# A decoder layer on one core: the first tap of a convolution on ACT, the bias table mirrored by transfers through memory, and small parameters made elsewhere

## The reference, cut to what matters

```python
proj = jnp.einsum('bsd,de->bse', x, w_in[l])
z, xbc, dt_raw = proj[..., :o_z], proj[..., o_z:o_xbc], proj[..., o_xbc:o_dt]
...
xbc = jax.nn.silu(causal_dwconv(xbc, conv_w, conv_b))            # 4 taps, each channel by itself
dt = jax.nn.softplus(dt_raw.astype(jnp.float32) + dt_bias.astype(jnp.float32))
a = -jnp.exp(a_log.astype(jnp.float32)) * dt
...
bias = rel_bias.astype(jnp.float32)[t5_bucket(jnp.maximum(dist, 0))]   # dist = q - k
logits = jnp.where(dist >= 0, logits + bias.transpose(2, 0, 1)[:, None], -jnp.inf)
...
lam = (jnp.exp(jnp.sum(lq1 * lk1)) - jnp.exp(jnp.sum(lq2 * lk2)) + lam_init)
```

## Time and profile before

| | |
|---|---|
| median of 3 runs | 1021.77 us (1020.12 to 1022.16) |
| the profiled execution's own time | 1021.97 us |
| its span | 1019.8 us |
| PE busy in the span | 993.3 us, 97% |
| DVE busy | 524.5 us, 51% |
| ACT busy | 376.4 us, 37% |
| POOL busy | 56.3 us, 6% |
| DMA | 290.85 MB, mean 285 GB/s |

### The profile page before, as it was taken

One profiled execution on the slowest core, in us unless ns is written; L12 is line 12 of the kernel. 1 busy time (PEld: TensorE's weight loads), 2 busy tenths in 40 slices (PEclk: granted clock), 3 DMA queues, 4 the chain that ended last, 5 costly groups with the idle time before them and its releaser, 6 DMA issues.

```text
span 1019.8 us, 15454 instructions
## 1 busy us (share of the span) xinstructions
PE 993.3 (97%) x6370; PEld 711.6 (70%) x6371; DVE 524.5 (51%) x1049; ACT 376.4 (37%) x687; POOL 56.3 (6%) x53
## 2 busy tenths in 40 slices
PE   8999999999999999999999999999999999999994
PEld 7998999999999999998974444444444444444432
DVE  6899455675769966855677222322223222222223
ACT  5665435556577744455321211121112111211112
POOL 0000202324200000000010000000000000000000
PEclk9999999999999999999999999999999999999998
DMA  8564534333344555658837999999999999999972
GB/s 305 188 226 146 185 123 167 124 125 125 125 166 166 181 192 182 233 207 350 347 141 280 419 419 421 420 419 420 420 418 420 420 420 420 421 420 419 420 326 83
DMA packets 41653, 290.85 MB, mean 285 GB/s; under 512 B 4712, under 2 KB 5872, under 8 KB 6896
## 3 DMA queue, kind: packets, MB, share of 16 engines
q1 hardware_dynamic: 40800, 284.62, 70.6%
q0 software_dynamic: 784, 5.24, 1.3%
HBM read 288.78 MB, written 1.06 MB: 284 GB/s over the span
## 4 chain that ended last, share of the span: by engine, by line
PE 86%; DVE 10%; issue 2%; DMA 1%; ACT 1%; SPq 0%; ACTq 0%; DVEq 0%
PE stream L1548 24%; PE stream L1876 22%; PE stream L1900 11%; PE stream L1573 8%; PE work L1865 6%; DVE w_lo L972 3%; DVE acc L1008 3%; PE stream L1824 2%; PE stream L1828 1%; PE stream L1826 1%; PE stream L1830 1%; DMA raw<-in_wdense 1%; PE work L1675 1%; PE work L1651 1%; PE work L1851 1%
## 5 line engine op out<-in xcount | busy, mean ns | idle before, releaser
L972 DVE TENSOR_TENSOR w_lo<-raw,w_hi 128x1024 fp32r<-128x1024 f32 x142 | 171.4, 1227 | 57.1 <-ACT w_hi L668 57.0
L1876 PE MATMUL stream<-ring,xg 128*64 128x512 f32 x640 | 197.0, 592 | 0.8 <-issue 0.8
L668 ACT ACTIVATE w_hi<-raw 128x1024 fp32r<-128x1024 f32 x142 | 147.1, 1052 | 53.2 <-DMA raw<-in_wdense 36.4
L1548 PE MATMUL stream<-xT_hi,w_hi 128*128 128x256 f32 x560 | 161.3, 288 | 1.4 <-DVE w_lo L972 1.4
L1548 PE MATMUL stream<-xT_lo,w_hi 128*128 128x256 f32 x560 | 158.6, 283 | 0.0
L1548 PE MATMUL stream<-xT_hi,w_lo 128*128 128x256 f32 x560 | 158.4, 283 | 0.0
L1876 PEld LDWEIGHTS stream<-ring,xg 128*64 128x64 f32 x640 | 63.0, 137 | 91.5 <-issue 90.4
L1548 PEld LDWEIGHTS stream<-xT_hi,w_hi 128*128 128x128 f32 x560 | 106.8, 191 | 6.1 <-issue 3.3
L1548 PEld LDWEIGHTS stream<-xT_lo,w_hi 128*128 128x128 f32 x560 | 106.5, 190 | 0.3 <-issue 0.2
L1548 PEld LDWEIGHTS stream<-xT_hi,w_lo 128*128 128x128 f32 x560 | 106.6, 190 | 0.0
L1425 DVE TENSOR_TENSOR hh<-h,stream 128x256 f32<-128x256 f32 x32 | 13.5, 421 | 172.3 <-ACT h L901 172.3
(11 more groups left out here) (381 smaller groups left out, 2038.1 us busy)
## 6 DMA issues: line engine op xcount, KB each, us to landing
ring<-in_wstream SPq DMA_DIRECT2D x120, 1024.0 KB, 16.1
raw<-in_wdense SPq DMA_DIRECT2D x73, 1024.0 KB, 4.9
place_e<-in_wstream SPq DMA_DIRECT2D x24, 1024.0 KB, 17.1
place_m<-in_wstream SPq DMA_DIRECT2D x12, 1024.0 KB, 14.8
place_c<-in_wstream SPq DMA_DIRECT2D x12, 1024.0 KB, 16.4
place_w<-in_wstream SPq DMA_DIRECT2D x12, 1024.0 KB, 16.0
place_x<-in_wstream SPq DMA_DIRECT2D x12, 1024.0 KB, 17.6
ln<-in_lnp POOLq DMA_DIRECT2D x3, 1024.0 KB, 7.1
```

The lines of the kernel that those rows point to most:

```text
L668: nc.scalar.activation(w_hi[:, q % ROUNDED, :], raw[:, q % 6, :], ACT.Copy).then_inc(w_rounded, 1)
L972: tt(w_lo[:, q % 6, :], raw[:, q % 6, :], w_hi[:, q % ROUNDED, :].bitcast(F32), ALU.subtract).then_inc(w_rest, 1)
L1548: last = mm(S[n % 4][:, 0:SEQ], w[:, b, :], a[:, kb, :], start=(kb + j == 0), stop=(kb == chunks * KB - 1 and j == len(parts) - 1))
L1876: last = mm(S[2][e * SLOTS:(e + 1) * SLOTS, :], feature_block(buf, kb)[:, col + e * SLOTS:col + (e + 1) * SLOTS], tiles[e][kb // 4][:, kb ...
```

## The change

- The first tap is made by ACT, right after it has copied the block, before it rounds the next chunk (semaphore `conv_begun`). DVE makes the other three.
- `four_ident` is made by three additions on GpSimd (`bands_ready`) in place of a reduction on DVE.
- The dot products of lambda move on DVE behind the copy of dt, and ACT's two small exponentials move behind block 1 of `q`, next to the exponential of dt. DVE's two steps that follow them move as well.
- The bias rows go to memory (`rel_rows`), are copied in memory to 128 rows of each head (`rel_scratch`), and are read with a pitch of 383 elements into `rel`. The flip matmuls, ACT's four copies and the tile `rel_flipped` are gone, and DVE waits for the transfer before the first logits.
- `decay_end`'s matmul and exponential come one block earlier or so.

```diff
@@ SP
                 if m == 7:
                     sp.wait_ge(rel_cp, 1)
-                    sp.dma_start(rel_scratch, bds[0:DIFF_HEADS, :]).then_inc(rel_ld, 16)
+                    sp.dma_start(rel_rows, bds[0:DIFF_HEADS, :]).then_inc(rel_ld, 16)
                 if m == 8:
                     sp.wait_ge(rel_ld, 16)
-                    sp.dma_start(rel_flipped[:],
-                                 bass.AP(rel_scratch.tensor, 0, [[1, P], [384, DIFF_HEADS], [1, SEQ]])
+                    sp.dma_start(rel_scratch.rearrange("h r j -> r h j"), rel_rows.unsqueeze(0).to_broadcast([P, DIFF_HEADS, 384])
+                                 ).then_inc(rel_ld, 16)
+                if m == 12:
+                    sp.wait_ge(rel_ld, 32)
+                    sp.dma_start(rel[:],
+                                 bass.AP(rel_scratch.tensor, P - 1, [[383, P], [384 * P, DIFF_HEADS], [1, SEQ]])
                                  ).then_inc(rel_ld, 16)
@@ POOL
             pool.wait_ge(small_in, 48)
+            for band in range(1, 4):
+                so_far = four_ident[:] if band > 1 else ident[:, 0:SSD_HEADS]
+                if band > 1:
+                    pool.wait_ge(bands_ready, band - 1)
+                nc.gpsimd.tensor_tensor(four_ident[:], so_far, ident[:, band * SSD_HEADS:(band + 1) * SSD_HEADS], ALU.add
+                                        ).then_inc(bands_ready, 1)
@@ ACT
-                leave("xbc", b, xpad[:, b % 4, CONV - 1:PADDED])
+                leave("xbc", b, xpad[:, b % 4, CONV - 1:PADDED], then_round=False)
+                act.wait_ge(act_took, b + 1)
+                if b >= 2:
+                    act.wait_ge(conv_silu, b - 1)
+                nc.scalar.activation(acc[:, b % 2, :], xpad[:, b % 4, 0:SEQ], ACT.Copy, scale=conv_w[:, b, 0:1]
+                                     ).then_inc(conv_begun, 1)
+                round_chunks(out_index("xbc", b))
                 if b >= 1:
                     conv_act(b - 1)
-                if b == 8:
-                    act.wait_ge(small_in, 48)
-                    act.wait_ge(lam_dots, 2)
-                    nc.scalar.activation(exp_alog[:], row[:, R_ALOG:R_ALOG + SSD_HEADS], ACT.Exp
-                                         ).then_inc(small_exp, 1)
-                    nc.scalar.activation(lam_e[:], lam_d[:], ACT.Exp).then_inc(small_exp, 1)
...
                 if h == 1:
+                    act.wait_ge(small_in, 48)
+                    nc.scalar.activation(exp_alog[:], row[:, R_ALOG:R_ALOG + SSD_HEADS], ACT.Exp
+                                         ).then_inc(small_exp, 1)
+                    act.wait_ge(lam_dots, 2)
+                    nc.scalar.activation(lam_e[:], lam_d[:], ACT.Exp).then_inc(small_exp, 1)
                     act.wait_ge(dt_pre, 1)
...
-            for k in range(4):
-                act.wait_ge(flip_mm, k + 1)
-                nc.scalar.activation(rel[:, 2 * k:2 * k + 2, :], W[k][:].rearrange("p (h k) -> p h k", h=2), ACT.Copy
-                                     ).then_inc(flip_cp, 1)
@@ DVE
-                ve.wait_ge(small_exp, 2)
-                link(stt(neg_lam[:], lam_e[:, 1:2], -LAM_INIT, lam_e[:, 0:1], ALU.add, ALU.subtract))
-                link(ts(exp_alog[:], exp_alog[:], -1.0, None, ALU.mult))
-                link(nc.vector.tensor_reduce(four_ident[:], ident.rearrange("p (g h) -> p h g", g=4), AX.X, ALU.add))
...
-                ve.wait_ge(act_took, b + 1)
-                if b >= 2:
-                    ve.wait_ge(conv_silu, b - 1)
-                link(ts(acc[:, b % 2, :], xpad[:, b % 4, 0:SEQ], conv_w[:, b, 0:1], None, ALU.mult))
+                ve.wait_ge(conv_begun, b + 1)
...
             nc.vector.tensor_copy(dtT[:], W[1][:, 0:SEQ]).then_inc(dtT_cp, 1)
+            lambda_products()
...
-            ve.wait_ge(flip_cp, 4)
+            ve.wait_ge(rel_ld, 48)
@@ PE
-            for h in range(6):
+            for h in range(5):
                 feature_major("k", h, xT_r)
-            pe.wait_ge(rel_ld, 32)
             pe.wait_ge(rel_cp, 1)
             pe.wait_ge(a_done, 1)
-            for k in range(4):
-                mm(W[k][:], flip, rel_flipped[:, 2 * k:2 * k + 2, :], start=True, stop=True).then_inc(flip_mm, 1)
-            feature_major("k", 6, xT_r)
-            pe.wait_ge(flip_cp, 4)
             mm(W[0][:, 0:SSD_HEADS], strict, a_v[:, 0, :], start=True, stop=True).then_inc(end_mm, 1)
+            for h in range(5, 7):
+                feature_major("k", h, xT_r)
```

More of the change, by code:

```diff
@@ L231, in layer_kernel @@
         rel = sb("rel", [P, DIFF_HEADS, SEQ], G)
-        rel_flipped = sb("rel_flipped", [P, DIFF_HEADS, SEQ], H)
         ln1 = sb("ln1", [P, 2, D], Z + 8 * KIB)
@@ L329, in layer_kernel @@
         strict = cs[:, C_STRICT:C_STRICT + P]
-        flip = cs[:, C_FLIP:C_FLIP + P]
         ones = cs[:, C_ONES:C_ONES + P]
@@ L343, in layer_kernel @@
         w_router = cs[:, C_WR:C_WR + KB * EXPERTS].rearrange("p (k e) -> p k e", k=KB)
-        rel_scratch = nc.dram_tensor("rel_scratch", [DIFF_HEADS, 384], F32, kind="Internal").ap()
+        rel_rows = nc.dram_tensor("rel_rows", [DIFF_HEADS, 384], F32, kind="Internal").ap()
+        rel_scratch = nc.dram_tensor("rel_scratch", [DIFF_HEADS, P, 384], F32, kind="Internal").ap()
         conv_in = sem("conv_in")
@@ L363, in layer_kernel @@
         rel_mm = sem("rel_mm")
-        flip_mm = sem("flip_mm")
         dt_mm = sem("dt_mm")
@@ L438, in layer_kernel @@
         rel_cp = sem("rel_cp")
+        conv_begun = sem("conv_begun")
         conv_done = sem("conv_done")
+        bands_ready = sem("bands_ready")
         lam_dots = sem("lam_dots")
@@ L716, in _ @@
                 leave("k", h, kT[:, h, :])
-            for k in range(4):
-                act.wait_ge(flip_mm, k + 1)
-                nc.scalar.activation(rel[:, 2 * k:2 * k + 2, :], W[k][:].rearrange("p (h k) -> p h k", h=2), ACT.Copy
-                                     ).then_inc(flip_cp, 1)
-            leave("k", 6, kT[:, 6, :])
             act.wait_ge(end_mm, 1)
             nc.scalar.activation(decay_end[:], W[0][:, 0:SSD_HEADS], ACT.Exp).then_inc(small_exp, 1)
+            leave("k", 6, kT[:, 6, :])
             leave("k", 7, kT[:, 7, :])
@@ L988, in small_parameters, with lambda_products @@
                 nc.vector.tensor_copy(bds[0:DIFF_HEADS, :], W[0][0:DIFF_HEADS, 0:384]).then_inc(rel_cp, 1)
+            def lambda_products():
                 for k in range(2):
@@ L1027, in _ @@
             ve.wait_ge(small_exp, 3)
+            link(stt(neg_lam[:], lam_e[:, 1:2], -LAM_INIT, lam_e[:, 0:1], ALU.add, ALU.subtract))
+            link(ts(exp_alog[:], exp_alog[:], -1.0, None, ALU.mult))
             link(ts(s, e, 2.0, None, ALU.add))
@@ L1600, in _ @@
                 if h == 1:
+                    pe.wait_ge(bands_ready, 3)
                     pe.wait_ge(dtT_cp, 1)
```

1 line of the change is left out of this document (removed).

## The result

| | before | after |
|---|---|---|
| median | 1021.93 us (4 runs, 1020.12 to 1022.16) | 1011.97 us (4 runs, 1011.01 to 1012.25) |
| the profiled execution's own time | 1021.97 us | 1012.25 us |
| its span | 1019.8 us | 1010.2 us |

The ratio is 0.9907, with a 95% interval of 0.9894 to 0.9921. The forecast was 1011.7 us, 1010.0 to 1015.0.

A forecast was written before the change was run, and what follows sets the result against it. PE was taken to bound the kernel, busy 97% of the span, so only its waits, slow clock and needless work count. 1.28 + 1.60 + 2.2 + 1.65 + 3.43 - 0.1 = 10.1 us off 1021.77 gave 1011.7, range 1010.0 to 1015.0.

The forecast's parts named there:

- the clock term: From 92 to 96 us, behind the wait for dt, the clock averages 0.57; without that wait 1.65 us are gained.
- pace of 2.85: In the `xbc` stage DVE's block falls from 2.96 to 2.58 us, so PE sets 2.85 us a block; gain 1.28.
- cover on ACT: ACT's two blocks with taps take about 4.6 of 5.7 us; about 1.1 us of its wait for weights remains, cost 0.
- hole at dt closing: PE's wait at 91.10 us for DVE's copy of dt vanishes as DVE no longer lags; gain 2.2 us.
- 1.60 to the exponentials: Moving the small parameters out of block 8 removes DVE's 4.09 us there and PE's hole at 49.38 us; gain 1.60.
- not in the median run: Rival: the median run before had no clock drop, or PE drops elsewhere; 8.4 us gained, 1013.3 us; chance 0.10.
- The copy in memory: Copying 1.57 MB behind weight tile 8 takes 5.5 to 11 us, cost 0; rival: it makes the kernel slower, chance 0.03.
- loss B - 6: With a copy of B us delaying weight tile 9, PE loses at most B - 6, from 0 to 5 us.
- 4 us of lead: In the `xbc` stage DVE's rest of a chunk (`w_lo`) is ready some 4 us before PE wants it.
- The flip's 3.43: The flip matmuls take 3.43 us on PE's own path; removing them gains 3.43.
- the change does nothing: Rival: the 10 us are lost further down, where the later stages are PE too; no change, chance 0.03.
- ACT becomes the bound: Rival: tap with its wait over 1.1 us, DVE lags, the dt hole and clock drop return; about 1016.7, chance 0.06.

The follow-up runs named there:

- the hole filled: The kernel before, with 16 matmuls whose result nobody reads put before PE's wait for the copy of dt; 1020.46 us, ratio 0.9995 to the kernel before.
- two and four copies: The changed kernel with the copy in memory made twice, or four times, the additional tables read by nobody; 1018.65 us and 1032.13 us.
- its own kernel: The changed kernel with the bias made as before, by flip matmuls on PE and copies on ACT; 1014.64 us, ratio 0.9938 to the kernel before.

## Why the prediction was right, and where it was not

**The sum.** Its order of reading held: PE's own work, PE's waits, the clock. The rests differ by 10.2 us, the sum was 10.1, the medians differ by 10.0. Both the profile and the median of before are of its upper group of times, see the clock term.

**Tap on ACT.** The pace of 2.85, the cover on ACT, and the hole at dt closing held, and the raw dt began at 79.78 us against 79 forecast, 0.6 of it the later start of block 2. The tap takes 0.51 us, not the 0.45 taken; it equals the silu's row, which like it reads an operand from memory. Of ACT's 1.1 us of wait said to remain, 0.84 to 1.27 was measured, but for the 3.62 behind the copy. DVE does not idle 0.3 us in each block for ACT's tap, as was said: from 15 to 130 us it waited for the tap twice, 0.7 us in all, and 11 times, 19.7 us in all, for `w_hi`. Its slack is real, but it waits for the weights. Such a wait at 57 us was named as a sign of being wrong if it reached PE; it did not.

**The terms were not independent.** This step failed, and that the total came out right in spite of it is because all the edits were made at once. The text booked 1.28 (pace) to the tap, 1.60 to the exponentials and 2.2 + 1.65 to the end of DVE's lag, as if each went with its own edit. All draw on one lead of DVE. Its two drains before were 0.11 us in each block and 4.09 once. With only one drain back the rest is 3.9 us (tap) or 0.8 (exponentials) longer, with both 7.3. So 1.28 + 1.60 + 2.2 + 1.65 = 6.7 is wrong for each part. For the pair it is near the 7.3, which hold two clock drops where the sum has one, and the 6.5 between the medians.

**The clock term.** It was in the sum with 1.65, and in the rivals with 0.10 for "not in the median run". The profiles show its size, 1.7 us; that the hole at dt brings it rests on one profile with the hole filled and on the upper group that is missing then. Whichever way the two groups come about, the median of before is 1020.7 or 1021.9 by the luck of a few runs, and that the measured difference, 10.0, is so near the forecast one of 10.1 is in part this luck. Against the later medians of 1020.7 the gain is 8.7 us, against the first 10.0. For the few runs that were shown, 0.10 was fair, since two of the three lie in the upper group; for a fresh measurement, 21 of 49 runs in the upper group make the smaller gain the likelier one. The Trainium skill (TensorE: Matmul & The Clock Gate, the part on the HAM clock gate) says that the watch on activity is not tied to the kernel's start. The two groups, and 1.54 us with a drop beside 1.59 us without, are compatible with that; no run here shows it.

**The copy in memory.** 6.1 us, inside the bounds of 5.5 and 11, and without cost. The loss B - 6 should have been B - 7.3 by the kernels with two and four copies, plus a clock drop once PE waits. The "4 us of lead" was right as what there is without the copy: 1.4 us are left of it with a tile that lands 7.4 us after its issue, 2.6 more than the median.

**The rest.** The flip's 3.43 is confirmed by its own kernel. GpSimd's three additions (0.42 us, then 2 x 0.48, done before 20 us) and the moved steps cost nothing. The logits of head 0 begin at 157.98 us, where they began at 167.54, and DVE has no wait for a DMA before them. That the change does nothing, or that ACT becomes the bound, is refuted by the profile after.

## What to carry to other kernels

When several edits relieve one engine that feeds another, keep one account of its lead over time, with every drain and every refill, and charge the consumer only with what exceeds it; a sum of edit by edit is right only when all are made. On top of a wait of TensorE, even one of the 1.5 to 2 us seen here, put the slowed stretch that may follow it, with a chance and not as a certainty. The time of a kernel may itself be two values, as before's is here, so look at how the single runs group before a difference of 1 to 2 us is explained.

## What the runs showed of the hardware

- A clock drop cost 1.7 us behind idle times of 1.54 us (at dt, tap back), 2.12 us (at dt, before) and 4.48 us (two copies) alike, and 3.2 us behind 17.72 us. Behind 1.43 us at 49 us before and 1.59 us at the same place with the hole at dt filled, the profiles had none. In the kernel after, whose PE has no hole between 45 and 120 us, there is none.
- The start differs between executions: 32 plain matmuls took 9.65 us in the profile after and 7.29 in that with the exponentials back, and block 2 began at 15.90 and 14.51 us. The changed kernel alone has 15.90 and 15.35 in its two profiles. That is up to 1.4 us between executions whose PE has the same matmuls up to there.
- A copy within memory of 12 KB to 1.57 MB, in packets of 1536 bytes, took 6.1 us (257 GB/s written, and as much read), two took 12.0 and four 25.2. A load of weights issued behind them on the same queue landed later with each: 7.4, 13.4 and 19.9 us after its issue, where 4.8 is the median. Behind four, SP issued it at 57.83 us, after 11.21 us in the issues of the copies themselves.
